# A two-layer hybrid attention trunk: latent attention with heads in sets of four, and the gated linear readout with tokens on partitions

## The reference

```python
h = rmsnorm(x, norm_g)
(qa, ka, va, ga, qb, kb, vb, ab, gb, cq, ckv, kr, gc, mg) = split_cols(h @ w_in)
# A: sliding-window attention, 8 heads over 2 key/value heads
ya = swa_sink_attention(rope(qa), rope(ka), va, a_sinks) * silu(ga);  za = ya @ w_oa
# B: gated linear attention, 4 heads, key 64, value 128, chunks of 64 tokens
log_a = log_sigmoid(ab @ w_alpha + b_alpha) / 16
S_c = exp(g_end) * S_{c-1} + (k * exp(g_end - g))^T v;   o_t = q_t S_c        # per chunk c
yb = rmsnorm(o, b_head_g) * silu(gb);                                       zb = yb @ w_ob
# C: latent attention, 8 heads, nope 64 + rope 32, value 64, chunk-causal
q_c = rmsnorm(cq) @ w_uq;  kv = rmsnorm(ckv) @ w_ukv
s = (q_nope . k_nope + q_rope . k_rope) * 96 ** -0.5, masked;  p = softmax(s)
yc = (p @ v_c) * silu(gc);                                                  zc = yc @ w_oc
y = sigmoid(mg_0) * za + sigmoid(mg_1) * zb + sigmoid(mg_2) * zc
x = x + y @ w_out
```

## Time and profile before

| | |
|---|---|
| median of 3 runs | 1009.23 us (1008.88 to 1009.68) |
| the profiled execution: its own time, its span | 1008.85 us, 1007.0 us |
| PE busy | 992.1 us (99% of the span), 5168 matmul records |
| DVE busy | 624.7 us (62%) |
| ACT busy | 427.3 us (42%) |
| granted clock of TensorE, mean | 0.997 |

### The profile page before, as it was taken

How to read it: one execution, slowest core, us unless ns; L and a number is a source line. 1 busy time by engine, 2 the same in 40 slices (tenths; PEclk the granted TensorE clock), 3 DMA queues, 4 the chain that set the end, 5 groups by cost and what they waited for, 6 DMA issues and landing times.

```text
span 1007.0 us, 13335 instructions
## 1 busy us (share of the span) xinstructions
PE 992.1 (99%) x5168; PEld 792.8 (79%) x5168; DVE 624.7 (62%) x1142; ACT 427.3 (42%) x804; POOL 1.6 (0%) x6
## 2 busy tenths in 40 slices
PE   8999999999999999999999999999999999999996
PEld 6878878887777877788888887888877787767885
DVE  7746448546647576666556655584575667765844
ACT  6343335425542355533435333542354424554323
POOL 0000000000000000000000000000000000000000
PEclk9999999999999999999999999999999999999998
DMA  7323311322135211022223332122221522111212
GB/s 261 124 70 132 125 64 65 123 86 84 64 105 146 84 63 62 37 75 101 95 77 118 105 119 84 67 101 105 84 79 69 154 102 80 43 49 58 96 51 84
DMA packets 29952, 92.93 MB, mean 92 GB/s; under 512 B 3825, under 2 KB 6129, under 8 KB 29762
## 3 DMA queue, kind: packets, MB, share of 16 engines
q1 hardware_dynamic: 27362, 88.07, 24.7%
q10 hardware_dynamic: 2528, 4.02, 1.6%
HBM read 86.24 MB, written 3.28 MB: 89 GB/s over the span
## 4 chain that ended last, share of the span: by engine, by line
PE 91%; ACT 3%; DVE 3%; issue 1%; DMA 1%; SPq 0%; POOLq 0%; POOL 0%; ACTq 0%; DVEq 0%
PE ring L569 72%; PE nat L569 5%; PE nat L740 3%; PE nat L750 3%; PE nat L777 2%; ACT w_hi L793 1%; PE nat L763 1%; PE nat L703 1%; PE nat L726 1%; DVE w_lo L1095 1%; DMA raw<-pieces 1%; PE nat L691 0%; ACT gates L1042 0%; SPq L445 0%; PE aux L665 0%
## 5 line engine op out<-in xcount | busy, mean ns | idle before, releaser
L569 PE MATMUL ring<-act_hi,w_hi 128*128 128x512 f32 x848 | 348.8, 411 | 1.1 <-DVE w_lo L1095 0.9
L569 PE MATMUL ring<-act_hi,w_lo 128*128 128x512 f32 x848 | 331.1, 390 | 0.0
L569 PE MATMUL ring<-act_lo,w_hi 128*128 128x512 f32 x848 | 330.9, 390 | 0.0
L793 ACT ACTIVATE w_hi<-raw 128x1024 fp32r<-128x1024 f32 x153 | 161.5, 1057 | 340.2 <-PE ring L569 308.7
L1095 DVE TENSOR_TENSOR w_lo<-raw,w_hi 128x1024 fp32r<-128x1024 f32 x153 | 186.4, 1219 | 54.2 <-ACT w_hi L793 54.1
L569 PEld LDWEIGHTS ring<-act_hi,w_hi 128*128 128x128 f32 x848 | 159.3, 188 | 45.8 <-issue 11.8
L569 PEld LDWEIGHTS ring<-act_hi,w_lo 128*128 128x128 f32 x848 | 159.2, 188 | 34.4
L569 PEld LDWEIGHTS ring<-act_lo,w_hi 128*128 128x128 f32 x848 | 159.5, 188 | 32.6 <-issue 1.9
L1402 DVE SCALAR_TENSOR_TENSOR gates<-ring,rstd 128x512 f32<-128x512 f32 x72 | 49.7, 690 | 115.8 <-PE ring L569 115.2
L569 PE MATMUL ring<-y_hi,w_hi 128*128 128x512 f32 x192 | 74.8, 390 | 0.4 <-DVE bank_a L1490 0.4
L569 PE MATMUL ring<-y_hi,w_lo 128*128 128x512 f32 x192 | 74.7, 389 | 0.0
(11 more groups left out here) (193 smaller groups left out, 1041.3 us busy)
## 6 DMA issues: line engine op xcount, KB each, us to landing
raw<-pieces SPq DMA_DIRECT2D x153, 512.0 KB, 3.5
xt<-x_t SPq DMA_DIRECT2D x8, 256.0 KB, 6.0
bank_a<-work SPq DMA_DIRECT2D x32, 64.0 KB, 2.0
out_t<-gates SPq DMA_DIRECT2D x7, 256.0 KB, 2.3
rope<-tables SPq DMA_DIRECT2D x1, 1024.0 KB
bank_g<-k_rope_dram ACTq DMA_DIRECT2D x2, 512.0 KB, 4.2
q_rope_dram<-work ACTq DMA_DIRECT2D x4, 256.0 KB, 2.2
bank_a<-q_rope_dram ACTq DMA_DIRECT2D x4, 256.0 KB, 6.2
```

The source lines that it names most:

```text
L569: mm = pe.matmul(dst, stationary, moving, start=start and i == 0, stop=stop and i == 2)
L793: nc.scalar.activation(w_hi[:, n % HL, :], raw[:, n % RAW, :], ACT.Copy).then_inc(hi_split.sem, 1)
```

## The change

Pieces keep their number, size and order, and the quarters of the projections are the same.

- **Branch C in sets.** A step is four heads and one query tile: 8 sets a layer. Nope channels are packed so that 32 of them for each of four heads fill the 128 partitions; a set's scores are three parts (nope, nope, rope) of 32 rows for each of four heads, accumulated in the head's own bank, all four `nat` banks at once (now one tensor, `quad`). The turned probabilities go back to the same four banks. So the scores of a set wait until the four copies of the set ahead are out, and the copies wait for the values of the set ahead. The values now go to the bank `aux`.
- **Ring banks.** Keys are emptied by one DVE copy of 128 rows, queries by one ACT copy; the rope rows are spread by SP (4 and 16 small DMAs a layer) straight from SBUF for the queries.
- **Branch B.** `gla_state` and `gla_read` are one block each; in the read, 64 x 64 of `q_b` is stationary and 128 columns of the state move, so tokens lie on partitions. Squares are added up on DVE, one Ln and one Exp on 128 x 16 serve all heads, DVE scales the four banks, and PE turns them back with 16 transposes (`gla_turn`), four quarters after `gla_norm`.
- **The start.** First halves of pieces 0 and 1 come early, and PE alternates between the two pieces.

```diff
     step(("tanh", 0), ("gla_state", 0))
-    half(g + 1, 0)
-    step(("gla_state", 1))
...
+    half(g + 2, 0)
+    step(("gla_read", 0))
     half(g + 2, 1)
-    step(("tanh", 2), ("silu", 1))
+    step(("tanh", 2), ("silu", 1), ("gla_sum", 0))
     piece(g + 3)
-    step(("tanh", 3), ("silu", 2))
-    for q in range(4):
-        step(("gla_read", q), ("quarter", 4 * m + q))
+    step(("tanh", 3), ("silu", 2), ("gla_norm", 0))
+    half(m, 0)
     step(("silu", 3))
...
+    half(m, 1)
+    step(("tanh", 4), ("gla_turn", 0))
...
+    quarters(8)
+    for y in range(2 * TT):
+        qt = y // 2
+        todo.append(("score_c", y))
+        if y > 0:
+            todo.append(("value_c", y - 1))
+        quarters(1)
+        todo.append(("divide_c", y))
+        quarters(1)
+        if y > 0 and y % 2 == 0:
+            todo.append(("y_hi", TT + qt - 1))
+        quarters((1, 1, 2, 3)[qt])
+        if y > 0 and y % 2 == 0:
+            todo.append(("y_lo", TT + qt - 1))
+        todo.append(("turn_c", y))
+        quarters(1)
...
                     elif name == "score_c":
-                        mm = pe.matmul(nat[i % 2][:, 0:n], q_c[0:C_DH, h, qt * P:(qt + 1) * P],
-                                       k_c[0:C_DH, h, 0:n], start=True, stop=True)
+                        pe.wait_ge(turn_out.sem, turn_out.at(layer, NA + 4 * i))
+                        for part in range(3):
+                            for a in range(4):
+                                rows = slice(32 * a, 32 * a + 32)
+                                q, k = ((q_n[rows, g, part, ts], k_n[rows, g, part, 0:n]) if part < 2 else
+                                        (q_r[rows, g, ts], k_r[rows, 0:n]))
+                                mm = pe.matmul(nat[a][:, 0:n], q, k, start=part == 0, stop=part == 2)
...
+                    elif name == "turn_c":
+                        for a in range(4):
+                            pe.wait_ge(divided.sem, divided.at(layer, NA + 4 * i + a + 1))
+                            for b in range(i // 2 + 1):
+                                mm = pe.transpose(nat[a][:, b * P:(b + 1) * P], prob_c[a][:, b * P:(b + 1) * P], ident)
+                            mm.then_inc(turn_done.sem, 1)
...
                     elif name == "gla_read":
-                                mm = pe.matmul(nat[2 * pair + h][:, cs], state[half, c, pair, :], q_b[half, pair, cs],
+                                    mm = pe.matmul(nat[2 * (t // 2) + r][64 * c:64 * c + 64, col:col + B_DV],
+                                                   q_b[rows, pair, cs], state[rows, 2 * t + c, pair, :], start=True, stop=True)
...
+                    elif name == "gla_turn":
+                        for k, h in enumerate(HEAD_ORDER):
+                            pe.wait_ge(head_nat.sem, head_nat.at(layer, 2 if k < 2 else 4))
+                            for t in range(TT):
+                                mm = pe.transpose(nat[h][:, t * P:(t + 1) * P], o_nat[2 * (t // 2) + r][:, col:col + B_DV], ident)
...
-                                nc.scalar.activation(k_c[0:64, o + 1, :], ring[(first_output(p) + o + 1) % 3][64:128, :],
-                                                     ACT.Copy).then_inc(ring_act.sem, 1)
...
-                                nc.scalar.activation(q_c[0:64, h + 1, :], ring[(first_output(p) + o) % 3][64:128, :],
-                                nc.vector.tensor_copy(q_c[0:64, h, :], ring[(first_output(p) + o) % 3][0:64, :]
+                                nc.scalar.activation(q_n[:, g, f, :], ring[(first_output(p) + o) % 3][:, :],
...
+                jobs = [(p, k) for p in range(2) for k in range(2)] + [(p, k) for k in range(2, KT) for p in range(2)]
```

More of the change, by code:

```diff
@@ L65, in first_output, with act_reads @@
     return sum(outputs_of(q) for q in range(p))
+def act_reads(p, o):
+    return (p == PUKV and o % 2 == 0) or (p, o) == (PUQ, 2) or p == PUQ + 1
 def by_act(r):
     return sum(first_output(p) + o < r for p in (PUKV, PUQ, PUQ + 1) for o in range(outputs_of(p)) if act_reads(p, o))
[L73 to L80, removed]
 def by_dve(r):
-    return r - sum(first_output(PUKV) + o < r for o in range(0, 8, 2))
+    return r - by_act(r)
 def emptied_by(r):
[L90 to L94, removed]
+    by_scalar = by_act(r + 1) > by_act(r)
+    return not by_scalar, by_scalar
 def signals_before(p):
@@ L167, in make_schedule @@
     step(("tanh", 0), ("gla_state", 0))
-    half(g + 1, 0)
-    step(("gla_state", 1))
-    half(g + 1, 1)
-    step(("tanh", 1), ("silu", 0), ("gla_state", 2))
+    piece(g + 1)
+    step(("tanh", 1), ("silu", 0))
     half(g + 2, 0)
-    step(("gla_state", 3))
+    step(("gla_read", 0))
     half(g + 2, 1)
-    step(("tanh", 2), ("silu", 1))
+    step(("tanh", 2), ("silu", 1), ("gla_sum", 0))
     piece(g + 3)
-    step(("tanh", 3), ("silu", 2))
-    for q in range(4):
-        step(("gla_read", q), ("quarter", 4 * m + q))
+    step(("tanh", 3), ("silu", 2), ("gla_norm", 0))
+    half(m, 0)
     step(("silu", 3))
[L181 to L196, removed]
+    half(m, 1)
+    step(("tanh", 4), ("gla_turn", 0))
+    for k in range(B_HEADS):
+        half(m + 1 + k // 2, k % 2)
+        if k % 2:
+            step(("tanh", 5 + k // 2))
+        step(("gla_out", k), ("gla_hi", k))
+        if k > 0:
+            step(("gla_lo", k - 1))
+    half(m + 3, 0)
+    step(("gla_lo", B_HEADS - 1))
+    half(m + 3, 1)
+    step(("tanh", 7))
+    for j in range(4, 8):
+        piece(m + j)
+        step(("tanh", 4 + j))
     def quarters(n):
@@ L330, in build_hybrid_trunk @@
         prob, prob_t = [work[:, i, :] for i in range(3)], [work[:, 3 + i, :] for i in range(4)]
+        prob_c, prob_ct = [work[:, i, :] for i in range(4)], [*(work[:, 4 + i, :] for i in range(3)), bank_a[:, 3072:3584]]
         k_dec = bank_g[:, 0:1024].rearrange("p (t n) -> p t n", t=TT)
@@ L632, in _ @@
                         continue
+                    if name == "quarter" and layer == 0 and i // 4 < 2:
+                        if i == 0:
+                            first_pieces()
+                        continue
                     if name == "quarter":
@@ L638, in _ @@
                         aux_bank(layer, u)
+                        pe.wait_ge(o_read.sem, o_read.at(layer, 0))
                         pe.wait_ge(setup_loaded.sem, SETUP)
@@ L1270, in _ @@
                             ALU.subtract).then_inc(aux_free.sem, 1)
-                    elif name == "gla_read" and i == 3:
-                        for h in range(2):
-                            head_square_lo(layer, h)
                     elif name == "latent_norm":
```

521 lines of the change are left out of this document (264 added, 257 removed).

## The result

| | before | after |
|---|---|---|
| median of 4 runs, us | 1009.45 (1008.88 to 1009.75) | 987.08 (986.96 to 987.57) |
| profiled execution: span, us | 1007.0 | 985.3 |
| PE busy, us | 992.1 | 970.7 |

The ratio is 0.9781, with a 95% interval of 0.9769 to 0.9793. The changed kernel is 22.4 us faster; 993.0 was predicted, within 986 to 1002. The direction and the mechanism are right, and the gain is 6 us larger than the sum said.

What follows compares the result with a forecast made beforehand. PE, busy for 99% of the span, was taken as the bound; 2 x (3.4 + 3.1 + 1.3 - 1.0 + 0.7) + 1.2 = 16.2 us off 1008.85 gave 992.6, as median 993.0, range 986 to 1002.

Steps and rivals of the forecast that it cites:

- What bounds: Whole kernel: PE works for 99% of the span, so neither ACT nor DVE can bound it; PE's instruction time counts.
- Four row groups at once: Branch C scores: four 32-row groups overlap fully, 14.5 us a layer for 17.6, gain 3.1.
- Rival 1: Branch C scores: row groups overlap in part, sets cost 18.2 us a layer for 14.5, total 1000; chance 0.14.
- rival 2: Branch C scores: two row groups at a time or fewer, slower; total 1017, or 1070 at one; chance 0.08.
- but not below 0.054 us a record: Branch C scores: floor from the readout's 128-column weight load, making a set of 128 columns 1.30 us.
- Forms: Branch C: 25 changes between full-array and tiled form for 32, at 0.185 us each; gain 1.3 us a layer.
- Waits of the sets: Branch C: only the scores after the fifth set wait, for ACT's copies; loss 1.0 us a layer, bounds 0.6 and 1.5.
- rival 3: Branch C: PE waits 1 us more in each of 16 sets; total 1009, no change; chance 0.06.
- Branch B: States, readout, norm and 16 transposes: 6.57 us a layer for 9.98, including a 0.65 wait; gain 3.4.
- rival 4: The readout's block and the starts gain nothing: 6 us later, total 999; chance 0.06.
- Key and query pieces: Two PE waits for a ring bank go, as ACT alone empties these banks; gain 0.7 us a layer, bounds 0 and 1.
- The start: Once: waits between pieces 0 and 1 are filled, each tile of x feeding six matmuls; gain 1.2 us, bounds 0 and 2.

Runs made afterwards that it cites:

- the second experiment: Changed kernel plus probe blocks of 32-row matmuls, 128-column weights, added once in layer 0, 18 full matmuls between; 0.112, 0.056, 0.038, 0.029 us a record on one to four row groups.

## Why the prediction was right, and where it was off

*What bounds.* Right: PE was and is busy for 99%, and every term could be read off its timeline. The median lies near the low end of the range, and nearly all of the misses have one sign, so luck did not put it there. Taking a step's price from the distance between two projections around it, instead of from busy times, gave the sizes.

*Four row groups at once.* Right at 256, 384 and 512 columns (1.33, 1.97 and 2.61 us a set, for 1.32, 1.98 and 2.64 forecast). Rival 1 (overlap in part, 3.5 at 512) and rival 2 (two at a time, 5.3) are refuted by these sets, and the count of row groups in the second experiment shows why: one, two, three and four groups give 0.112, 0.056, 0.038 and 0.029. By that count the fourfold packing is worth 3.9 here at 128 columns (0.112 to 0.029), and not the 3.07 that the Trainium skill ("TensorE: Matmul & The Clock Gate", Part 3) gives at 512 columns; at 512 a record of the sets is 0.109, a quarter of the 0.44 of the earlier trace rows, though one row group of 32 was not measured there. (One sum of rival 2 is off: 22.6 us a layer is 2.3 groups at once, by its own 52.8 for one at a time, and not 2.6.) The time of the readout was rightly attributed to the load and not to a lack of overlap.

*The step that failed* is in the scores: "but not below 0.054 us a record". The load of 128 columns is no floor that stays when groups are added. The two sets of 128 columns took 0.70 for 1.30, 1.2 us a layer and 2.4 in all. The number was right for two row groups; it should have been read as 0.107 divided by two, and 0.027 set as the bound for four.

*Forms.* Right in kind: seven changes fewer a layer. A change measured 0.21 in branch C for 0.185, some 0.2 us a layer by that price; the blocks themselves also fit 0.185, so this share is an estimate.

*Waits of the sets.* The wait was foretold in the right place and for the right reason, at 0.64 a layer for 1.0, within its bounds; no other set waits, so rival 3 is refuted. The rest of branch C's surplus is PE's wait for ACT's copies in before (0.5, in two waits, by the line under the result) and what was not traced further, about 0.2 us a layer.

*Branch B.* Right in sum. States and readout take 2.11 each for 2.10. The transposes with their wait take 2.61 for 2.37, since the wait with its restart is about 0.9 and not 0.65. The price before was low too, 10.1 for 9.98, so the blocks gained 3.3 and the shift 3.4. With the blocks apart 4.4 us were lost again, where rival 4 would have lost none.

*Key and query pieces.* Right (0.7 for 0.85 each layer), with the cause shown: the half copy of DVE costs 0.9 us a layer when it comes back. The list of waits shows 0.2 of it; the rest are longer distances between matmuls, as in the earlier trace rows.

*The start.* Undersized, 1.2 for 2.1. The step counted the waits between pieces 0 and 1 and left out those between the first tiles of x. Before, the distances between PE's matmuls from 7.44 to 10.23 exceed 0.2275 by 1.2 in sum; after, from 7.08 on, by 0.4, and the first matmul itself is 0.36 earlier. 0.8 was lost again behind the first norm, to a `w_lo` that DVE made late, and 0.6 came back when the wait for another at 41.5 us went.

So 5.6 us were missed: 2.4 by the load, 0.9 by the start, 0.7 by the wait of the sixth set, 0.3 by the pieces, and some 1.3 by the forms and the small waits of before in branch C.

## What to carry to other kernels

When fp32 matmuls use only part of the rows, the price of a record is the longer of its load and its stream, divided by the number of tiles that take turns: two or four row groups with weights of 128 columns, and four tiles of 64 x 64. That is an estimate that fits every block measured here within 0.01 us. Before the sum, work out that quotient for the new number of tiles, and don't carry over an old one as a floor. Put neighbours on different row groups: this order alone was worth 30 us here. On an engine that is always busy, small blocks of another form are paid by the change (0.2 us each way), so join them, and after a wait is removed look at once for the operation behind it on the next engine. When several moves go into one run, check each by the shift of the blocks around it; here the total agreed while three of four terms did not.

## What the runs showed of the hardware

- Weight loads overlap over row groups like streams do. A record with 128-column weights and 64 or 128 moving columns takes 0.110 us on the full array, 0.056 on two row groups of 64 rows, and 0.027 to 0.029 on four of 32.
- In 64 x 64 tiles, four of them in turn, a record takes 0.014 us with 64-column weights and 64 moving columns, and 0.027 with 128 moving columns.
- The overlap depends on the order of issue: 0.029 in turn, 0.043 two by two, 0.070 three by three at 128 columns; 0.055 and 0.122 at 256.
- Going from the full array to row groups or tiles, or from one such form to another, cost 0.18 to 0.21 us on PE.
- PE's clock went from 2.4 to 1.2 GHz while PE was busy for the whole time, but with blocks of matmuls on small parts of the array from 223.5 to 238.3 us, the last on one row group; it was back at 248.5, behind a block of 64 x 64 tiles and three full matmuls. With 18 full matmuls between such blocks it stayed at 2.4. In the last norm it fell at 977.8, after four matmuls had been all of PE's work since 974.6, and the next four took 2.07 us for 1.16.
